# A fused block with a 32-expert MoE: last tile's routing, the bias product in visit 16, a new transfer order in the last visit

## The chip, the cores and the metric

The kernel runs on one core of a Trainium2 chip. The metric is device time in microseconds (us), the median of three runs.

## The reference

One transformer layer in float32, 512 tokens (`SEQ`) of 1024 channels, followed by a final RMS norm:

```
mix = concat(gated_delta_net(h), conformer_conv(h))      h = RMSNorm(x)
x   = x + mix @ w_out
xn  = RMSNorm(x)
x   = x + moe(xn)
out = RMSNorm(x) * final_norm_w

moe: logits = xn @ w_router + b_router;  top 4 of 32, gates = softmax(top values)
     for each token and each of its four experts e:
       gate, up = split(xn @ w_gate_up[e] + b_gate_up[e])
       gate = min(gate, 7); up = clip(up, -7, 7)
       y   += gate_e * (((up + 1) * gate * sigmoid(1.702 * gate)) @ w_down[e] + b_down[e])
```

Each expert has 8 MB of gate and up weights and 4 MB of down weights, which is 403 MB over the 32 experts.

## The kernel before

**The part ahead of the experts** (0 to about 370 us) computes the two mixers. Its last stage is the output projection, `outp`, over four tiles of 128 tokens (t = 0 to 3). PE interleaves it with `xn_turn(t)`, which transposes a finished tile, and `logits(t)`, the router product. For each tile DVE adds the residual (`residual`), ACT takes the norm (`x2_square`, `x2_rstd`), DVE multiplies it in (`normed`, L1386) and picks the top four (`route`): a mask of 32 columns for each token, built by four chained compares (L1410). POOL writes the normed tile to `xn_rows` in DRAM (L613) and splits the gates into three bf16 parts (`split`, L599 to L607).

**Row numbers.** After tile 3, a scan over the masks of all tiles gives each choice's rank among its token's four, a product with a triangular matrix gives its place among its expert's tokens (L2117, L2120), and `hot(e)` compares the places of expert e with the slot numbers (L1502). `idx_mm(e)` multiplies these one-hot matrices by a table of token numbers, gate parts and ranks (L2130), so that DVE's `numbers` gets, for each of 128 slots of the expert, a row of `xn_rows`, a row of the results in DRAM and a gate. It publishes them with `idx_ready`, the queue entry of DVE at L1541. POOL then gathers four groups of 32 slots (`gather`, L624), and DVE transposes what has landed (`first_turn`, `xt_turn`). The semaphore `first_in` counts the first two gathers, `gathered` the others.

**Visits.** An expert is a visit, i = 0 to 31. `gate_up(i)` works in four pairs of weight rows (c = 0, 2, 4, 6) that lie in eight 1 MB slots of `ring`; visit 0 has the rows 4 and 5 in other buffers (`EARLY`). `down(i-1)`, four units (u = 0 to 3) in `dslots`, follows in visit i, so the down work of an expert is done one visit later. After pair 4 PE computes the numbers of visit i+2; visit 1's come after pair 0 of visit 0. DVE turns the result of the products, adds bias and clips; ACT takes the sigmoid (`sigmoid_gate`) and copies the older down results with their gates to `yb` (`results`); POOL scatters them to `y_rows`, four planes of 512 rows in DRAM, one for each rank. Visits 1 to 30 are one loop on each engine. The variable `m` is 30.

**Order of the transfers.** SP issues all weight transfers in a fixed order, each behind a wait on the counter of its buffer: `gu_used` for ring slots, `d_used` for down units. A wait in this queue holds all that stands behind it. SP also waits for `xn_out`, the landing of all normed tiles, ahead of pair 4 of visit 1.

**The last visit.** PE turns the gates (`gates_turn`, L2141) and adds the down bias as a product of gates and `b_down` (`routed_bias(t)`, L2152, with `add_bias(t)` on DVE). These four steps stand behind pair 0, pair 2, the older down units and pair 4. SP issues pairs 0 and 2, both older down pairs, pairs 4 and 6, the last expert's down rows into ring slots 0 to 3, and then the planes back from `y_rows`: the first and second into `dslots` (they need the older down units done), the third into ring slots 4 and 5 (it needs pair 6 and the older scatters), the last into slots 6 and 7 after the last scatters. DVE adds the planes to `hbuf` (L1720), ACT and DVE take the final norm, SP stores. ACT loads the final norm row behind its last results.

## Time and profile before

| | |
|---|---|
| median of 3 runs | 1390.28 us (1388.48 to 1390.84) |
| the profiled execution | 1390.32 us, span 1388.6 us |
| PE matmul busy | 1232.1 us (89%) |
| PE weight load busy | 540.9 us (39%) |
| DVE busy | 683.6 us (49%) |
| ACT busy | 220.4 us (16%) |
| POOL busy | 327.2 us (24%) |
| moved by DMA | 455.33 MB, 328 GB/s in the mean |

The page cuts the span into 40 slices of 34.7 us. The rate of the DMA engines is 252, 339, 401, 410 and 418 GB/s in slices 11 to 15 (347 to 521 us), 424 to 427 in nearly all from 16 to 37, and 379, 409 and 248 in the last three.

How to read it: a busy engine is not by that the one that sets the time. PE is 89% busy over the span, and in the middle the DMA engines are full as well. Which of the two waits for the other is seen in the idle time ahead of a group and in the depth of the queue, the time from the issue of a transfer to its landing. The chain of waits is followed back from the last instruction, so it holds what released each step. In the trace the queue entries of an engine (SPq, DVEq) are its semaphore and DMA instructions.

### The profile page before, as it was taken

Reading aid. Unit: us, or ns where it says so; the run is one execution under the profiler, and the core shown is the slowest. Engines: PE = TensorE matmul, PEld = TensorE weight load, DVE = VectorE, ACT = ScalarE, POOL = GpSimd, SP = SyncE. Lnnn points to the kernel's source line nnn. Section 1 sums busy time; section 2 is a strip of 40 time slices with the busy share of each in tenths; the row PEclk is TensorE's granted clock in tenths of the full one; section 3 lists DMA queues with packets and bytes.
Section 4 is the critical chain, followed back from the end, with each engine's and each line's share of the span. In section 5 each row is a group of like instructions: output and inputs, shape, how many; then the busy total and the mean of one; then the engine's idle time right before and its main releaser. Section 6 shows DMA issues by size and latency. Waiting matters only on the chain.

```text
span 1388.6 us, 32055 instructions
## 1 busy us (share of the span) xinstructions
PE 1232.1 (89%) x12818; PEld 540.9 (39%) x12819; DVE 683.6 (49%) x1365; ACT 220.4 (16%) x435; POOL 327.2 (24%) x435
## 2 busy tenths in 40 slices
PE   6999999999599999799899899788987887879992
PEld 3444555564234443244433334233432332334331
DVE  2898884444543453436433334445443334354428
ACT  3125545313100010000010000000100000001103
POOL 6002111001222233222323222222222222222221
...
GB/s 307 87 61 92 1 31 1 201 73 46 252 339 401 410 418 424 425 427 426 425 426 424 424 427 427 424 427 425 425 424 426 425 426 427 426 425 425 379 409 248
DMA packets 58142, 455.33 MB, mean 328 GB/s; under 512 B 12060, under 2 KB 22356, under 8 KB 32982
## 3 DMA queue, kind: packets, MB, share of 16 engines
...
q14 instruction: 12, 0.10, 0.0%
...
## 4 chain that ended last, share of the span: by engine, by line
PE 53%; DMA 36%; DVE 7%; issue 2%; ACT 2%; POOL 1%; SPq 0%; POOLq 0%; DVEq 0%; ACTq 0%
DMA ring<-in_w_gate_up_dram 26%; PE bank L2166 23%; PE bank L2219 11%; DMA dslots<-in_w_down_dram 8%; PE bank L1826 6%; PE bank L2017 4%; DVE dslots L1145 2%; PE bank L1821 2%; DVE hbuf L1720 1%; PE bank L1894 1%; PE bank L1901 1%; DMA rows<-in_x_dram 1%; DMA wq<-xn_rows,idx_in 1%; PE bank L2152 1%; PE bank L1982 1%
## 5 line engine op out<-in xcount | busy, mean ns | idle before, releaser
L2166 PE MATMUL bank<-ring,wq 128*32 128x512 f32 x4992 | 561.2, 598 | 69.6 <-DMA ring<-in_w_gate_up_dram 66.9
L2166 PEld LDWEIGHTS bank<-ring,wq 128*32 128x32 f32 x4992 | 167.8, 110 | 422.7 <-issue 419.7
L2219 PE MATMUL bank<-dslots,intra 128*32 128x256 f32 x5056 | 281.7, 380 | 24.8 <-DMA dslots<-in_w_down_dram 24.6
L2219 PEld LDWEIGHTS bank<-dslots,intra 128*32 128x32 f32 x5056 | 165.0, 110 | 151.4 <-issue 53.9
L1533 DVE TENSOR_REDUCE small<-bank 128x4 f32<-128x8 f32 x33 | 5.5, 166 | 415.7 <-PE bank L2130 415.7
L1012 ACT ACTIVATE zrows<-intra 128x1024 f32<-128x1024 f32 x31 | 32.8, 1058 | 796.8 <-DVE intra L1626 796.8
L1826 PE MATMUL bank<-hbuf,ring 128*128 128x512 f32 x320 | 148.5, 604 | 0.1
L619 POOL COPY idx_in<-idx 128x4 int32 (+1 forms) x32 | 11.9, 371 | 557.8 <-DVE wq L1511 535.4
L1598 DVE STREAM_TRANSPOSE wq<-bank 128x512 f32<-128x512 f32 x124 | 77.8, 685 | 71.0 <-PE bank L2166 71.0
L624 POOL DMA_INDIRECT wq<-xn_rows,idx_in x82 | 101.7, 1241 | 44.2 <-POOL idx_in L619 27.8
L629 POOL DMA_INDIRECT y_rows<-rows,idx_out x79 | 81.2, 1027 | 55.8 <-issue 43.6
L1145 DVE SCALAR_TENSOR_TENSOR dslots<-dslots,small 128x512 f32<-128x512 f32 x120 | 89.3, 778 | 0.8 <-DVE small L1114 0.2
L1826 PEld LDWEIGHTS bank<-hbuf,ring 128*128 128x128 f32 x320 | 57.3, 190 | 59.3 <-issue 56.3
L1511 DVE STREAM_TRANSPOSE wq<-wq 128x1024 f32<-128x1024 f32 x31 | 63.2, 2040 | 12.6 <-DMA wq<-xn_rows,idx_in 12.6
L1006 ACT ACTIVATE rows<-bank,small 128x256 f32<-128x256 f32 x124 | 48.5, 474 | 93.7 <-PE bank L2219 93.7
L2017 PE MATMUL bank<-ring,dslots 128*128 128x512 f32 x128 | 60.7, 608 | 0.1
L636 POOL DMA_DIRECT2D spare<-in_gdn_dt_bias_dram x93 | 51.8, 566 | 0.1
L1638 DVE SCALAR_TENSOR_TENSOR intra<-zrows,intra 128x1024 f32<-128x1024 f32 x31 | 38.0, 1225 | 27.9 <-PE bank L2219 27.2
L1619 DVE TENSOR_TENSOR zrows<-wq,small 128x256 f32<-128x256 f32 x124 | 44.1, 418 | 0.0
L1502 DVE TENSOR_SCALAR rows<-slot_no,small 128x512 bf16<-128x512 bf16 x136 | 39.1, 351 | 9.8 <-DVE place L1537 9.4
L1619 DVE TENSOR_TENSOR intra<-wq,small 128x256 f32<-128x256 f32 x124 | 43.1, 408 | 0.0
L556 POOL TENSOR_TENSOR sqbuf<-qkbuf 128x512 f32<-128x512 f32 x8 | 11.3, 1416 | 114.2 <-DVE qkbuf L1187 114.2
...
## 6 DMA issues: line engine op xcount, KB each, us to landing
ring<-in_w_gate_up_dram SPq DMA_DIRECT2D x127, 2048.0 KB, 24.9
dslots<-in_w_down_dram SPq DMA_DIRECT2D x61, 2048.0 KB, 25.4
...
dslots<-y_rows SPq DMA_DIRECT2D x2, 2048.0 KB, 20.2
rows<-in_x_dram SPq DMA_DIRECT2D x4, 512.0 KB, 9.8
hbuf<-in_x_dram SPq DMA_DIRECT2D x4, 512.0 KB, 5.5
```

The lines of the kernel that those rows point to most:

```text
L624: pool.indirect_dma_start(out=xg[:, g, :], out_offset=None, in_=xn_q, in_offset=bass.IndirectOffsetOnAxis(ap=numbers[:, g:g + 1], axis=0), ...
L629: pool.indirect_dma_start(out=y_q, out_offset=bass.IndirectOffsetOnAxis(ap=numbers[:, g:g + 1], axis=0), in_=y[:, g, :], in_offset=None, b ...
L636: pool.dma_start(spare[0:1, k * H:(k + 1) * H], gdn_dt_bias[0:1, :]).then_inc(done, 16)
L1006: ins = A(yb[:, g, :], bank[4 + g // 2][:, (g % 2) * QD:(g % 2 + 1) * QD], ACT.Copy, scale=gates[:, bass.ds(stage * GROUPS + g, 1)])
L1145: own.mark(V.scalar_tensor_tensor(out=cacc[:, j, :], in0=ubuf[:, j, k:k + SEQ], scalar=PT[:, j, k:k + 1], in1=cacc[:, j, :], op0=ALU.mult, ...
L1511: V.transpose(xT.rearrange("p g (c s) -> p g c s", c=KC), xg.rearrange("p g (r c) -> p g c r", c=KC)).then_inc(xt_ready, 1)
L1598: V.transpose(hidT[:, g, :, :].rearrange("p h (c s) -> p h c s", c=KC), bank[g][:, :].rearrange("p (h r c) -> p h c r", h=2, c=KC)).then_i ...
L1619: V.tensor_tensor(out[:, g, :].rearrange("p (b s) -> p b s", b=KC), hidT[:, g, half, :].rearrange("p (b s) -> p b s", b=KC), bias.to_broad ...
L1826: ins = M(bank_of(s)[:, :], unit_ap(u)[:, c, half * P:(half + 1) * P], hT[:, c, :], start=(c == 0), stop=(c == KC - 1))
L2017: ins = M(pair[half][:, :], lhs, w, start=(kc == 0), stop=(kc == KC - 1))
L2166: ins = M(bank[g][GROUP * j:GROUP * (j + 1), :], x[:, g, c * GROUP:(c + 1) * GROUP], w[:, :, j * QD:(j + 1) * QD], start=(c == 0), stop=(c ...
L2219: ins = M(b[GROUP * j:GROUP * (j + 1), col:col + QD], actT[:, g, c * GROUP:(c + 1) * GROUP], w[:, cc, j * QD:(j + 1) * QD], start=(c == 0 ...
```

## The change

**Last tile.** Residual and transposition of tile 3 go by halves, and DVE copies both halves of the turned tile, which ACT did for one. The 32 logits come out of one product with `fold_e` instead of a transposition and a reduction on DVE. The mask is one compare over four planes and one reduction with max. Ranks are scanned for each tile, places and one-hot matrices of tiles 0 to 2 are computed ahead of tile 3's norm, and the numbers of visit 0 come from products of three columns (`first_rows`), with the gates in products of their own later (`first_gates`). The rank is now column 2 of the table, the gate parts are columns 3 to 5. In the order listings an index stands ahead of a row as a rule; it is left out here.

**Start of visit 0.** ACT's queue writes the last normed tile to DRAM, counted by `wr_in`. The first gather alone counts `lead_in`; PE starts visit 0 with group 0 (`row_turned`), then group 1, then the others. `split(3)` stands behind the gathers, `hot(1)` behind the first transpositions, and `idx_mm(1)` behind pair 2. SP no longer waits for `xn_out`. SP's queue behind the output projection; L400 and L403 are pairs of gate and up rows, L411 and L414 a down unit, L407 and L410 a down pair. Before:

```order
L422 DMA wq<-in_w_gate_up_dram 128x2048
L400 DMA ring<-in_w_gate_up_dram 128x4096 [waits op_done]
L400 DMA ring<-in_w_gate_up_dram 128x4096 [waits xn_out1,xn_out0]
L411 DMA dslots<-in_w_down_dram 128x2048 [waits gathered,first_in]
L407 DMA dslots<-in_w_down_dram 128x4096
L360 TENSOR_LOAD n_iter [waits route_ready]
```

And now:

```order
L425 DMA wq<-in_w_gate_up_dram 128x2048
L403 DMA ring<-in_w_gate_up_dram 128x4096 [waits op_done]
L403 DMA ring<-in_w_gate_up_dram 128x4096
L414 DMA dslots<-in_w_down_dram 128x2048 [waits gathered,first_in,lead_in]
L410 DMA dslots<-in_w_down_dram 128x4096
L363 TENSOR_LOAD n_iter [waits route_ready]
```

The second ring transfer, pair 4 of visit 1, has lost its wait; the down rows of visit 0 keep theirs. Next PE, from the last logits to the row numbers of visit 1; the outputs `bank` are PSUM banks, `sqbuf` is the gathered and turned input of visit 0. Before:

```order
L2117 MATMUL bank<-kbg,count 128x32 [waits gate_ready]
L2117 MATMUL bank<-kbg,count 128x32 x9
L2120 MATMUL bank<-kbg,count 128x32 x4
L2130 MATMUL bank<-rows 128x6 [waits hot_ready,tg_ready]
L2130 MATMUL bank<-rows 128x6 x15
...
L2166 MATMUL bank<-ring,sqbuf 32x512 [waits slot_in0,xt_ready]
L2166 MATMUL bank<-ring,sqbuf 32x512 x7
...
L2130 MATMUL bank<-rows 128x6 [waits hot_ready,idx_ready]
```

And now:

```order
L2183 MATMUL bank<-rows 128x3 [waits hot_ready]
L2183 MATMUL bank<-rows 128x3 x11
L2104 MATMUL bank<-kbg,count 128x32 [waits gate_ready]
L2104 MATMUL bank<-kbg,count 128x32 x3
L2200 MATMUL bank<-kbg,count 128x32 x4
L2183 MATMUL bank<-rows 128x3 [waits hot_ready]
L2183 MATMUL bank<-rows 128x3 x3
...
L2232 MATMUL bank<-ring,sqbuf 32x512 [waits slot_in0,row_turned]
...
L2191 MATMUL bank<-rows 128x3 [waits tg_ready]
...
L2176 MATMUL bank<-rows 128x6 [waits hot_ready]
```

Behind the mask of tile 3 (`gate_ready`) stand four place products and four number products, where ten and 16 stood; the gates (L2191) and the numbers of visit 1 (L2176) stand inside visit 0, behind pair 0 and behind pair 2.

**Norm row and bias.** `b_down` is loaded after `route_ready` into the buffer of the norm weights, `finw` behind the first sigmoid. The loops are split at visit `MID` = 16, where gates_turn, the four bias steps (one behind each pair) and their adds stand; the numbers of visit 18 come behind them.

**Last visit.** The first two older down units are issued as two transfers behind pair 2, into `convbuf` and `qkbuf`, which are idle by then. PE does pairs 0 and 2, these two units, pairs 4 and 6, the other two units. The last activations go to `qkbuf` and wait for the first two units alone. `results` of the older expert stands between the second and third sigmoid of the last. SP's queue in the last visit (L454 and L460 are the last expert's down rows, the `y_rows` rows the planes). Before:

```order
L400 DMA ring<-in_w_gate_up_dram 128x4096 [waits gu_used]
...
L407 DMA dslots<-in_w_down_dram 128x4096 [waits d_used]
...
L407 DMA dslots<-in_w_down_dram 128x4096 [waits d_used]
...
L400 DMA ring<-in_w_gate_up_dram 128x4096 [waits gu_used]
...
L454 DMA ring<-in_w_down_dram 128x2048 [waits gu_used]
...
L462 DMA dslots<-y_rows 128x4x1024 [waits d_used]
...
L464 DMA dslots<-y_rows 128x4x1024 [waits landed]
...
L467 DMA ring<-y_rows 128x4x1024 [waits scattered]
```

And now:

```order
L452 DMA convbuf<-in_w_down_dram 128x2048
L452 DMA qkbuf<-in_w_down_dram 128x2048
...
L403 DMA ring<-in_w_gate_up_dram 128x4096 [waits gu_used]
...
L410 DMA dslots<-in_w_down_dram 128x4096 [waits d_used]
...
L460 DMA ring<-in_w_down_dram 128x2048 [waits gu_used]
...
L460 DMA ring<-in_w_down_dram 128x2048 [waits landed]
...
L465 DMA dslots<-y_rows 128x4x1024
...
L467 DMA ring<-y_rows 128x4x1024 [waits gu_used]
...
L470 DMA ring<-y_rows 128x4x1024 [waits scattered]
```

One older down pair has become two halves without a wait, the other stands behind pairs 4 and 6; the first plane follows the last down rows without a wait of its own, the second goes into ring slots 4 and 5, the third into 6 and 7.

The diff, cut to its core:

```diff
-        bdn = qkbuf[0:E, 0:D]
+        bdn = ffnw[0:E, :]
+        OLDER = [view(convbuf, 0, 2, D), view(qkbuf, 0, 2, D)]
+        actT_last = view(qkbuf, 0, GROUPS, KC * GROUP)
...
-        PLANES = [view(dslots, 0, T, D), view(dslots, 2 * SLOT, T, D), view(ring, 4 * SLOT, T, D),
-                  view(ring, 6 * SLOT, T, D)]
+        PLANES = [view(dslots, 0, T, D), view(ring, 4 * SLOT, T, D), view(ring, 6 * SLOT, T, D),
+                  view(dslots, 2 * SLOT, T, D)]
...
                 sp.dma_start(EARLY[c], rows_of(0, c)).then_inc(early_in, 16)
             sp.wait_ge(op_done, T)
             gate_up(0, 6)
-            for i in range(2):
-                sp.wait_ge(xn_out[i], 16 * T // 2)
             gate_up(1, 4)
-            sp.wait_ge(first_in, 32)
+            sp.wait_ge(lead_in, 16)
+            sp.wait_ge(first_in, 16)
...
             for c in range(0, KC, 2):
-                if c == 4:
-                    for u in (0, 2):
-                        sp.wait_ge(d_used, m * 4 + (u + 2))
-                        down_pair(None, u)
                 sp.wait_ge(gu_used, m * KC + (c + 2))
                 gate_up(E - 1, c)
+                if c == 2:
+                    for u in range(2):
+                        sp.dma_start(OLDER[u], down_rows(E - 2, u)).then_inc(slot_in[9], 16)
+            sp.wait_ge(d_used, m * 4 + 4)
+            down_pair(None, 2)
             for u in range(4):
-                sp.wait_ge(gu_used, m * KC + (KC + u + 1))
+                if u % 2 == 0:
+                    sp.wait_ge(gu_used, m * KC + (KC + u + 2))
+                if u == 1:
+                    sp.wait_ge(landed, m * 16 + 16)
                 sp.dma_start(view(ring, u * SLOT, 2, D), down_rows(E - 1, u)).then_inc(slot_in[u], 16)
...
-            sp.wait_ge(d_used, m * 4 + 8)
             sp.dma_start(PLANES[0], plane(0)).then_inc(plane_in[0], 16)
-            sp.wait_ge(landed, m * 16 + 16)
+            sp.wait_ge(gu_used, m * KC + (KC + 6))
             sp.dma_start(PLANES[1], plane(1)).then_inc(plane_in[1], 16)
             sp.wait_ge(gu_used, m * KC + 2 * KC)
...
                     split(t - 1)
-                pool.wait_ge(xn_ready, t + 1)
-                pool.dma_start(xn_dram[t * P:(t + 1) * P, :], xn[:, t % 2, :]).then_inc(xn_out[t % 2], 16)
+                if t < T - 1:
+                    pool.wait_ge(xn_ready, t + 1)
+                    pool.dma_start(xn_dram[t * P:(t + 1) * P, :], xn[:, t % 2, :]).then_inc(xn_out[t % 2], 16)
                 if 1 <= t < T - 1:
                     split(t - 1)
...
-                pool.wait_ge(xn_out[i], 16 * T // 2)
-            for g in range(2):
-                gather(g, idx, first_in)
+            pool.wait_ge(xn_out[0], 32)
+            pool.wait_ge(xn_out[1], 16)
+            pool.wait_ge(wr_in, 80)
+            gather(0, idx, lead_in)
+            gather(1, idx, first_in)
             for g in range(2, GROUPS):
                 gather(g, idx)
+            split(T - 1)
...
-            xnT_copy(3)
...
+            act.wait_ge(xn_ready, T)
+            act.dma_start(xn_dram[(T - 1) * P:T * P, :], xn[:, (T - 1) % 2, :]).then_inc(wr_in, 16)
...
+            act.dma_start(finw, final_norm_w.rearrange("(o d) -> o d", o=1).to_broadcast([P, D])).then_inc(
+                late_in, 16)
...
+            with act.Fori(1, MID) as i:
+                visit(i)
             act.wait_ge(gt_done, 1)
             A(GT, bank[7][0:E, :], ACT.Copy).then_inc(gt_copied, 1)
...
+            with act.Fori(MID, m + 1) as i:
+                visit(i)
...
+                if g == 2:
+                    act.wait_ge(d_used, m * 4 + 8)
+                    act.wait_ge(landed, m * 16 + 16)
+                    results((E - 2) % STAGES)
...
-            act.dma_start(finw, final_norm_w.rearrange("(o d) -> o d", o=1).to_broadcast([P, D])).then_inc(
-                late_in, 16)
...
-                own.mark(V.tensor_tensor(x2[:, t, 0:HALF], pair[0][:, :], x2[:, t, 0:HALF], ALU.add))
-                own.mark(V.tensor_tensor(x2[:, t, HALF:D], pair[1][:, :], x2[:, t, HALF:D], ALU.add))
-                own.settle()
-                dve.sem_inc(x2_ready, 1)
+                first = V.tensor_tensor(x2[:, t, 0:HALF], pair[0][:, :], x2[:, t, 0:HALF], ALU.add)
+                if t == T - 1:
+                    first.then_inc(x2_ready, 1)
+                V.tensor_tensor(x2[:, t, HALF:D], pair[1][:, :], x2[:, t, HALF:D], ALU.add).then_inc(x2_ready, 1)
...
-                own.mark(V.tensor_scalar(hits, iota_e, pr4[:, 0:1], None, ALU.is_equal))
-                for k in range(1, TOP_K):
...
-                ins.then_inc(gate_ready, 1)
+                own.mark(V.tensor_tensor(same, iota_e.rearrange("p (o e) -> p o e", o=1).to_broadcast([P, TOP_K, E]),
+                                         pr4.rearrange("p (k o) -> p k o", o=1).to_broadcast([P, TOP_K, E]),
+                                         ALU.is_equal))
+                own.settle()
+                V.tensor_reduce(Msk[:, t, :], same.rearrange("p k e -> p e k"), AX_X, ALU.max).then_inc(gate_ready, 1)
...
+            def ranks(t):
+                now = rank[:, t * E:(t + 1) * E]
+                dve.wait_ge(gate_ready, t + 1)
+                own.mark(V.tensor_tensor_scan(now, ones16[:, 0:E], Msk[:, t, :], 0.0, ALU.mult, ALU.add))
+                own.settle()
+                own.mark(V.tensor_scalar(view(tg, 0, T, E, 6)[:, t, :, 2:3].rearrange("p e o -> p (e o)"), now,
+                                         float(PAST), float(-PAST), ALU.mult, ALU.add))
...
+            hot_tile(0, 0)
+            hot_tile(0, 1)
...
+            dve.wait_ge(lgT_done, T - 2)
+            for half in range(2):
+                dve.wait_ge(xn_turned, T + half)
+                V.tensor_copy(xnT[(T - 1) % 2][:, 4 * half:4 * half + 4, :], view(bank[3 + half], 0, 4, P)
+                              ).then_inc(xnT_half, 1)
+            ranks(2)
+            places(2, 1, 2)
+            hot_tile(0, 2)
...
+            ranks(3)
+            places(3, 1, 3)
+            hot_tile(0, 3)
...
+            dve.wait_ge(idx_done, 1)
+            own.mark(V.tensor_reduce(rowf, first[:, :, 0:2], AX_X, ALU.add))
+            own.settle()
+            V.tensor_scalar(idx[:, 0:GROUPS], rowf, past, None, ALU.add).then_inc(idx_ready, 1)
...
+            dve.wait_ge(lead_in, 16)
+            first_turn(0, 1, row_turned)
+            dve.wait_ge(first_in, 16)
+            first_turn(1, 1, xt_ready)
             dve.wait_ge(gathered, 32)
-            first_turn(1)
...
+            base = (MID - 1) * LOOP_OWN + own.n
+            for t in range(T):
+                add_bias(t)
+            hid_turn(MID + 1)
+            rows_ahead(MID, base)
+            xt_turn(MID + 1)
+            act_part(MID, MID + 1, base + STEPS_IDX)
...
-            for t in range(T):
-                add_bias(t)
             dve.wait_ge(gu_used, m * KC + 2 * KC)
-            dve.wait_ge(d_used, m * 4 + 4)
...
-                if t == T - 1:
-                    pe.wait_ge(xnT_half, 1)
...
-                TR(bank[6][:, 0:P], lgT, ident).then_inc(lg_done, 1)
+                M(bank[6][:, 0:E], lgT, fold_e, start=True, stop=True).then_inc(lg_done, 1)
...
+            def places(t):
+                pe.wait_ge(gate_ready, t + 1)
+                for u in range(t + 1):
+                    ins = M(bank[1][:, t * E:(t + 1) * E], tri16 if u == t else ones16, Msk[:, u, :], start=(u == 0),
+                            stop=(u == t))
+                return ins
...
+            places(1).then_inc(pos_done, 1)
             logits_turn(2)
             outp(3, 12, 16)
+            places(2).then_inc(pos_done, 1)
...
+            def first_rows(t):
+                for g in range(GROUPS):
+                    ins = M(bank[0][:, 3 * g:3 * g + 3], ohv[:, t, g, :], tgv[:, t, 0, 0:3],
+                            start=(t == 0 and g == 0), stop=(t == T - 1), skip_group_check=True)
+                return ins
...
+            pe.wait_ge(hot_ready, T - 1)
+            for t in range(T - 1):
+                first_rows(t)
+            places(T - 1).then_inc(pos_done, 1)
+            for u in range(T):
+                ins = M(bank[7][:, 0:E], ones16, Msk[:, u, :], start=(u == 0), stop=(u == T - 1))
+            ins.then_inc(pos_done, 1)
+            pe.wait_ge(hot_ready, T)
+            first_rows(T - 1).then_inc(idx_done, 1)
...
                         for g in (1,) if by_bank else range(2):
                             ins = gu_mm(c, g, first)
-                        ins.then_inc(gu_used, 1)
+                        ins.then_inc(gu_used, 2 if first and c == 1 else 1)
                     if first and c0 == 0:
-                        pe.wait_ge(idx_ready, 1)
+                        first_gates()
+                    if first and c0 == 2:
                         idx_mm(1, 2 * T + 1)
...
+            pe.wait_ge(row_turned, 1)
...
+            tokens = tokens_left(pe, MID)
+            pe.wait_ge(xt_ready, MID + 2)
+            pe.wait_ge(idx_ready, MID + 2)
+            gates_turn()
+            for t in range(T):
+                gate_up(MID, pairs=(2 * t,), known=tokens)
+                routed_bias(t)
+            pe.wait_ge(acc_ready, T)
+            idx_mm(MID + 2, (MID + 3) * (T + 1) - 1)
+            older_down(MID)
...
-            routed_bias(0)
-            gate_up(m + 1, pairs=(2,), known=tokens)
-            routed_bias(1)
+            gate_up(m + 1, pairs=(0, 2), known=tokens)
             pe.wait_ge(act_ready, m + 1)
             pe.wait_ge(y_ready, m + 1)
-            down(m, tokens_left(pe, m))
-            routed_bias(2)
-            gate_up(m + 1, pairs=(4,), known=tokens)
-            routed_bias(3)
-            gate_up(m + 1, pairs=(6,), known=tokens)
+            older = tokens_left(pe, m)
+            down(m, older, range(2), {0: OLDER[0], 1: OLDER[1]})
+            gate_up(m + 1, pairs=(4, 6), known=tokens)
+            down(m, older, range(2, 4))
```

## Rows read from the trace of the kernel before

**Rows 1.** Windows: length, busy PE, PEld, DVE, ACT, POOL (count); clock; DMA share; GB/s.
```profile
404.00:1304.00 900.00, 807.35 (x9929) 327.75 (x9925) 377.67 (x764) 75.44 (x145) 238.32 (x292) 0.99 1.01 423
...
1316.00:1352.00 36.00, 34.50 (x372) 13.49 (x360) 8.65 (x13) 3.58 (x9) 8.92 (x14) 1.00 1.00 409
```

**Rows 2.** DMA issues (count, KB, us to landing): whole run, then 423 to 428 us.
```profile
ring<-in_w_gate_up_dram SPq DMA_DIRECT2D x127, 2048.0 KB, 24.9
...
dslots<-in_w_down_dram SPq DMA_DIRECT2D x1, 2048.0 KB, 10.0
```

**Rows 3.** Chain of waits (start, length, engine, output, line): routing to visit 1.
```profile
356.49 1.28 DVE convbuf L1386
...
360.27 0.25 DVE kbg L1410
...
361.99 1.24 DVE rows L1502 x4
...
364.63 0.03 DVEq L1541
...
367.09 2.86 DMA wq<-xn_rows,idx
...
371.12 7.67 PE bank L2166 x48
...
385.07 8.95 DMA wq<-xn_rows,idx_in
...
397.12 15.66 PE bank L2166 x144
```

**Rows 4.** Timeline (start, length, engine, line, operation, [idle before <-releaser]): SP, POOL.
```profile
352.57 9.71 SPq L400 DMA_DIRECT2D ring<-in_w_gate_up_dram  x2
...
358.07 0.57 POOL L613 DMA_DIRECT2D xn_rows<-convbuf  x1 [3.98 <-DVE convbuf L1386]
...
365.68 1.11 POOL L624 DMA_INDIRECT wq<-xn_rows,idx  x1 [2.87 <-issue]
...
381.11 1.02 POOL L624 DMA_INDIRECT wq<-xn_rows,idx_in  x1 [0.86 <-POOL idx_in L619]
```

**Rows 5.** DMA issues: the last normed tile (357 to 360 us), the final norm row.
```profile
xn_rows<-convbuf POOLq DMA_DIRECT2D x1, 512.0 KB, 3.8
...
rows<-in_final_norm_w_dram ACTq DMA_DIRECT2D x1, 512.0 KB, 5.7
```

**Rows 6.** Timeline of PE: first matmuls of a pair in visit 16.
```profile
867.03 3.64 PE L2166 MATMUL bank<-ring,wq 128*32 128x512 f32 x32 [1.01 <-DMA ring<-in_w_gate_up_dram]
```

**Rows 7.** Chain of waits: a bias step, older down units, pair 6 of the last visit.
```profile
1321.66 1.91 PE bank L2152 x4
...
1329.05 10.50 PE bank L2219 x192
...
1346.93 3.62 PE bank L2166 x32
```

**Rows 8.** Timeline of ACT, SP and DVE from the older results to the planes.
```profile
1339.70 1.57 ACT L1006 ACTIVATE rows<-bank,small 128x256 f32<-128x256 f32 x4 [19.83 <-PE bank L2219]
...
1340.13 0.41 SPq L464 DMA_DIRECT2D dslots<-y_rows  x1
1351.12 0.36 SPq L467 DMA_DIRECT2D ring<-y_rows  x1
...
1361.07 9.16 DVE L1720 TENSOR_TENSOR hbuf<-hbuf,dslots 128x1024 f32<-128x1024 f32 x8
...
1370.15 4.62 DVE L1720 TENSOR_TENSOR hbuf<-hbuf,ring 128x1024 f32<-128x1024 f32 x4
```

**Rows 9.** Windows: the last pair and the down units of visit 30.
```profile
1304.00:1316.00 12.00, 12.00 (x200) 6.37 (x196) 9.21 (x19) 1.06 (x1) 2.75 (x3) 1.00 0.72 294
```

**Rows 10.** DMA issues: second plane (1340 to 1341 us), third plane.
```profile
dslots<-y_rows SPq DMA_DIRECT2D x1, 2048.0 KB, 22.4
...
ring<-y_rows SPq DMA_DIRECT2D x1, 2048.0 KB, 17.0
```

216 lines of the change are left out of this document (111 added, 105 removed).

## The prediction

> **What bounds the kernel now.** I read the windows of the long middle first. From 404 us to 1304 us the 16 DMA engines are busy with a share of 1.01 and move 423 GB/s, while PE is busy 807 of 900 us; over 1316 to 1352 the share is again 1.00 [rows 1]. So from visit 2 on the stream of expert weights sets the pace. The issue rows say how deep its queue is: a pair of weight rows lands 10.0 us after its issue in visit 1, but 24.9 us in the median over the run [rows 2]; that is five transfers of 2 MB. Three things can therefore move the end: when the stream starts, how many bytes it carries, and what follows the last bytes. Work of PE, DVE or ACT in the middle is free as long as it is shorter than the queue.
>
> The chain of waits around routing tells when the stream starts [rows 3]. Residual, norm and router of tile 3 run in series, the norm at 356.49, the mask complete at 360.52, the row numbers published at 364.63; then two gathers, landed at 369.95, the turn and the first matmul at 371.12. PE is not the limit again until 397.12: visit 1's gathers take until 394.02. From there pairs are freed by PE and the stream is full. At the end [rows 7, 8] PE goes through routed bias and last visit until 1350.55, and DVE then adds planes without a pause from 1361.07.
>
> **The change, part by part.** The sum is made against the profiled execution, 1390.32 us (span 1388.6, so 1.7 outside), which is 0.04 above the median.
>
> *Last tile.* DVE copies half of the turned tile while it waits, which makes the logits some 1.0 us earlier, but rank, product and one-hot of tile 2 (some 1.2 us in five short operations) now stand ahead of the norm, which so starts at about 356.5 as before. After it the reduction of the logits goes (0.24 us) and four serial compares of 0.25 become one compare and one reduction of 0.28 each: 0.7 us. From mask to numbers took 4.1 us (360.52 to 364.63); a quarter of the scan, one one-hot instead of four (1.24 us for four [rows 3], so 0.9 less), four matmuls instead of 16, one reduction fewer and no place ahead of the numbers leave some 2.1 us. Numbers are ready at about 361.8, 2.8 us early. For tiles 0 to 2 the same work goes where DVE waits for PE.
>
> *What the gathers wait for.* They also need the last normed tile in DRAM. It is written at 358.07 and landed after 3.8 us, and SP held back pair 4 of visit 1 until then: its two issues span 352.57 to 362.28 [rows 4, 5]. Now both pairs, 4.2 MB, go at 352.6 and 352.9. At 423 GB/s, from a first byte near 353.4, they last until 363.3, and the 0.5 MB of the tile end with them at about 364.5. Bounds for the tile's landing: 3.8 us as before (361.7), and 8.95 us, which the gathers needed among weights [rows 3] (366.8); the norm row at the end, of the same size and among fewer transfers, took 5.7 us [rows 5]. I take 365.0. The first gather then goes at 366.0 against 365.68 [rows 4]: the 2.8 us are gone, +0.3.
>
> The Trainium skill (DMA: Bandwidth & Descriptors, "Queues, rings and completion order") says an engine empties a packet of some 9 to 17 descriptors of one ring before it turns to the next ring. No row here shows that order; it is the third rival below.
>
> *One gather opens visit 0.* Before, two had to land (369.95) and the turn took 1.2 us till PE started. Now one: 366.0, some 2.5 us to landing (2.86 for the second one before [rows 3]), 0.6 for half the turn: PE starts at 369.1, 2.0 us early. All four land at about 372.2, 0.3 late, and so do the down rows of visit 0 that SP queues behind that wait; nobody needs them before 418.
>
> *Visit 1's numbers move back.* Their 16 matmuls came after pair 0 (371.12 + 7.67 = 378.79 [rows 3]); now gates stand there (0.5 us) and they follow pair 2: 369.1 + 7.6 + 0.5 + 5.3 + 0.5 = 383.0, so visit 1's gathers are issued from 384.9 instead of 381.11 [rows 4], the last at 388.9. That speaks against the change. But the old ones landed at 394.02 only because weights drained till then: they are bounded by the drain, which ends about 1.5 us earlier, since pair 0's and pair 2's slots come free 1.5 to 2 us earlier. I take 392.5. Transposes and the first bank turn take 3.1 us as before (394.02 to 397.12): visit 1 starts at 395.6, **1.5 us early**. Bounds: PE's own path (369.1 + 24.2 + 0.5 + 1.2 = 395.0, a gain of 2.1), and a landing 8.95 us after the last issue (397.9, a start at 401.0, a loss of 3.9).
>
> *Final norm row in visit 1.* 0.5 MB, 1.2 us of the stream at 423 GB/s; visit 1 still has short pauses, so **+0.8** (bounds 0 and 1.2).
>
> *Bias in visit 16.* Four times 1.91 us [rows 7], 0.5 of transposes and 1.4 for the last add: 10 us of PE in visit 16. There PE waits for weights before each pair, 1.0 us in the row shown [rows 6], and transfers land some 24 us after issue, so the stream doesn't notice: 0. If the queue were dry it would be the full 10 us.
>
> *End.* The PE path loses 8.2 us of bias (1350.55 to 1342.4). It gains less, since weights then bind it. Transfers land there as the queue lets them: the second plane, issued at 1340.13, after 22.4 us, at 1362.5; the third, issued at 1351.12, after 17.0, at 1368.1, 5.6 us behind it [rows 8, 10]. The mean share falls to 0.72 between 1304 and 1316 [rows 9] although transfers are queued, so some engines are ahead and idle while others lag and never pause; filling the gap doesn't help those. Bytes and their number are the same in the new order (two halves, pairs 4 and 6, the second down pair, last down rows), so I keep the series, late by the 0.8. The last activation needs pair 6 (some 1340) and only down units 0 and 1, so DVE is through it by about 1352.5, where it was 1361.07: it now waits for planes. Plane 1 at 1363.3 plus four adds (4.6 us, [rows 8]) is 1367.9; plane 2 lands at 1368.1 + 0.8 - 1.2 (the norm row no longer runs beside it) = 1367.7. Third plane's adds start at 1367.9 against 1370.15: **-2.25**, the 0.8 within. Behind them the last plane, norm and store stay.
>
> The older results are 8 us later: down units 2 and 3 end at 1347.5 (5.25 us, half of [rows 7]), ACT copies till 1349.1; from the end of the copies (1341.27) to SP's third plane were 9.85 us [rows 8], so its issue is at 1359.0, ahead of 1362.5 when the plane before it lands. Covered by 3.5 us.
>
> Sum: -1.5 - 2.25 = -3.75: **1386.6 us**.
>
> **Rivals.** (2) *The start gains nothing.* Visit 1's gathers, issued 3.8 us later, land 1 to 4 us later than I say. Start 0 to +2, end -2.25: 1388.1 to 1390.1, say 1388.8. For: 8.95 us under load; against: their weights go earlier too. (3) *The tile's write passes pair 4.* If it follows pair 6 at once, it lands after 3.8 us as before, at 361.7, the first gather goes at 362.8, PE starts 5 us early and visit 1, then bound by its gathers, 4 us early: 1390.3 - 4.0 - 2.25 = 1384.1. That is what the skill's packets would give. Against: gathers of some KB took 8.95 us among weights. (4) *The lag is made up at the end.* The window from 1304 to 1316 leaves 0.28 of 12 us unused, 3.4 us [rows 9]; were it usable, planes landed that much earlier, and the third, issue bound, at about 1366: 1384.6. (5) *Slower: third plane too late.* Its issue hangs on down units 2 and 3, copies and scatters. If scatters take longer than 13.3 us instead of 9.85, each us is lost; if the plane needs 17.0 us from issue as before, it lands at 1376.0, DVE starts 5.9 us later than before, less 1.5: 1394.7. For: this chain moved by 8 us; against: the 17.0 us were queueing behind two planes. (6) *Visit 16 isn't hidden*: up to 10 us, 1396.6, if queue depth has shrunk below 10 us; 24 us speak against.
>
> **Chances.** Forecast 0.42, (2) 0.25, (3) 0.10, (4) 0.08, (5) 0.10, (6) 0.05. A measurement here can tell about 0.2% (2.8 us), so faster means below 1387.5. Three quarters of the forecast lie there (the bounds of the start reach across): 0.32 + 0.18 = 0.50. Same: 0.10 + 0.25 = 0.35; slower 0.15. Range: from between (3) and (4), 1383.8, to the slow end of (2) with the norm row at its full cost, 1390.8; (5), (6) and what lies below are left out.
>
> **What would show it.** Numbers ready near 361.8 but the first gather at about 366 (at 363 for rival 3); the first matmul at 369.1; visit 1 at 395.6; a share of 1.01 through visit 16 with bias matmuls in it; DVE waiting before each plane, its third set of adds at 1366.4 (1367.9 less 1.5). Wrong if the tile's write lands within 4 us of its issue, if visit 1 starts after 397.1, or if the third plane's issue comes after the second's landing.

## The result, and the profile after

The changed kernel takes 1393.58 us in the median of 18 runs (1391.3 to 1395.31), against 1390.32 for the kernel before (18 runs): a ratio of 1.0024, 95% interval 1.0017 to 1.0031. It is 3.3 us slower. I had forecast 1386.6, and a range that ended at 1390.8. The profiled execution took 1393.55 us, span 1391.8, so that it stands 3.2 us behind the one of before.

First the long middle. The windows of the changed kernel, columns as in [rows 1]:

```profile
404.00:1304.00 900.00, 817.59 (x9932) 323.80 (x9928) 382.31 (x769) 77.44 (x147) 239.17 (x292) 0.99 1.01 422
1304.00:1316.00 12.00, 12.00 (x176) 5.34 (x172) 6.96 (x16) 0.00 (x0) 0.17 (x1) 1.00 1.01 427
1316.00:1352.00 36.00, 30.18 (x410) 14.01 (x406) 13.29 (x31) 3.46 (x7) 7.97 (x12) 1.00 0.97 401
```

Share and rate are those of before in the middle; PE is busy 10 us longer in it, as the bias moved there. The time did not go there. The chain of waits from the last tile to visit 1 shows where it went [rows 3]:

```profile
357.04 8.82 DMA xn_rows<-convbuf
...
366.82 2.90 DMA wq<-xn_rows,idx
...
370.43 7.46 PE bank L2232 x48
...
389.96 5.33 DMA wq<-xn_rows,idx_in
```

The last normed tile took 8.82 us to land, in place of 3.8 [rows 5]. The row numbers were ready at 360.78, but the first gather, which also needs the tile, went at 366.82. PE started visit 0 at 370.43, 0.7 us earlier than before, and visit 1's last gather landed at 395.29, 1.3 us later. The timelines of SP and then PE over the same stretch and on to visit 2:

```profile
352.17 0.80 SPq L403 DMA_DIRECT2D ring<-in_w_gate_up_dram  x2
373.11 0.33 SPq L414 DMA_DIRECT2D dslots<-in_w_down_dram  x1
...
407.34 0.35 SPq L403 DMA_DIRECT2D ring<-in_w_gate_up_dram  x1
...
398.33 17.35 PE L2232 MATMUL bank<-ring,wq 128*32 128x512 f32 x144 [3.26 <-DVE wq L1625]
...
432.71 2.78 PE L2232 MATMUL bank<-ring,wq 128*32 128x512 f32 x24 [0.51 <-issue]
```

The same rows of the kernel before:

```profile
402.74 0.35 SPq L400 DMA_DIRECT2D ring<-in_w_gate_up_dram  x1
...
397.12 15.66 PE L2166 MATMUL bank<-ring,wq 128*32 128x512 f32 x144 [1.76 <-DVE wq L1598]
...
428.93 6.64 PE L2166 MATMUL bank<-ring,wq 128*32 128x512 f32 x60
```

Visit 1 starts 1.2 us late, its first 144 products take 1.7 us more, and visit 2 starts 3.8 us late (432.71 after 428.93). The other 0.9 us come behind these products: the older down units take 0.25 us more, and a pause of 0.51 us stands ahead of visit 2, for which the profile shows no releaser. The windows say why the products are slower (PE's granted clock is the third number from the end):

```profile
396.00:398.00 2.00, 0.00 (x0) 0.00 (x0) 2.00 (x3) 0.00 (x0) 0.00 (x0) 1.00 0.68 287
398.00:400.00 2.00, 1.67 (x12) 0.58 (x16) 1.96 (x6) 0.00 (x0) 0.00 (x0) 0.65 1.02 434
400.00:402.00 2.00, 2.00 (x16) 0.48 (x11) 1.81 (x9) 0.00 (x0) 0.79 (x2) 0.50 0.49 209
402.00:404.00 2.00, 2.00 (x24) 0.63 (x20) 1.97 (x6) 0.19 (x1) 1.64 (x2) 1.00 0.21 66
```

PE had been idle for 3.26 us. Its clock falls within the first of these products (0.65 is the mean of 398 to 400), is at 0.50, the 1.2 GHz level, until 402, and is back at 1.00, the 2.4 GHz level, after that. Before, the pause was 1.76 us and the clock stayed at 1.00. From visit 2 on the distance hardly changes: the numbers in visit 30 are computed at 1305.13 after 1301.34, 3.8 us apart.

Now the end. The lines are PE's timeline of the older down units 2 and 3, SP's issue of the third plane with its time to landing, and DVE's three sets of adds [rows 8, 10]:

```profile
1345.10 4.09 PE L2292 MATMUL bank<-dslots,intra 128*32 128x256 f32 x70 [1.11 <-DMA dslots<-in_w_down_dram]
1351.17 1.70 PE L2292 MATMUL bank<-dslots,intra 128*32 128x256 f32 x25 [1.98 <-issue]
...
1364.39 0.36 SPq L470 DMA_DIRECT2D ring<-y_rows  x1
...
ring<-y_rows SPq DMA_DIRECT2D x1, 2048.0 KB, 9.0
...
1359.98 4.63 DVE L1760 TENSOR_TENSOR hbuf<-hbuf,dslots 128x1024 f32<-128x1024 f32 x4 [1.60 <-DMA dslots<-y_rows]
1365.80 4.63 DVE L1760 TENSOR_TENSOR hbuf<-hbuf,ring 128x1024 f32<-128x1024 f32 x4 [1.20 <-DMA ring<-y_rows]
1373.38 4.63 DVE L1760 TENSOR_TENSOR hbuf<-hbuf,ring 128x1024 f32<-128x1024 f32 x4 [2.95 <-DMA ring<-y_rows]
```

DVE now waits ahead of each plane. The third set starts 3.2 us later than before (1370.15), which is the whole difference. Against a stream that is 3.8 us late, the new end has given back 0.6 us in this execution.

### The profile page after: what moved, and what is told of

It reads as the page before. It is cut to its first block, busy times and chain, and to the rows that moved or that the text cites. A ratio compares the mean times of both kernels' runs of the same rounds, so it can differ in the third digit from the quotient of the medians.

```text
span 1391.8 us, 32047 instructions
## 1 busy us (share of the span) xinstructions
PE 1236.1 (89%) x12838; PEld 534.9 (38%) x12839; DVE 682.6 (49%) x1359; ACT 220.6 (16%) x434; POOL 326.6 (23%) x434
## 4 chain that ended last, share of the span: by engine, by line
PE 55%; DMA 34%; DVE 5%; issue 3%; ACT 2%; POOL 1%; SPq 0%; POOLq 0%; DVEq 0%; ACTq 0%
PE bank L2232 24%; DMA ring<-in_w_gate_up_dram 20%; PE bank L2292 12%; DMA dslots<-in_w_down_dram 11%; PE bank L1866 6%; PE bank L2057 4%; DVE dslots L1154 2%; PE bank L1861 2%; PE bank L1934 1%; PE bank L1941 1%; DMA ring<-y_rows 1%; DMA xn_rows<-convbuf 1%; DMA rows<-in_x_dram 1%; PE bank L2218 1%; PE bank L2022 1%
## 5 line engine op out<-in xcount | busy, mean ns | idle before, releaser
L2232 PEld LDWEIGHTS bank<-ring,wq 128*32 128x32 f32 x4992 | 159.5, 111 | 419.4 <-issue 414.1
L1016 ACT ACTIVATE zrows<-intra 128x1024 f32<-128x1024 f32 x31 | 32.8, 1059 | 792.5 <-DVE intra L1653 740.5
```

The source lines that it names most:

```text
L2232: ins = M(bank[g][GROUP * j:GROUP * (j + 1), :], x[:, g, c * GROUP:(c + 1) * GROUP], w[:, :, j * QD:(j + 1) * QD], start=(c == 0), stop=(c ...
```

## The experiments

The kernel before was timed again beside each of the kernels below, and its median lay between 1389.2 and 1390.0 us. So where a microsecond matters, the ratio to it is compared and not the median. An interval is about 0.9 thousandths (1.2 us) to either side, 1.3 in e2, e6 and e8, which have the fewest runs. Rows and times within a run are from its one profiled execution.

**e1. SP's wait for the last tile put back** (on the changed kernel).

```diff
             gate_up(0, 6)
+            sp.wait_ge(xn_out[0], 32)
+            sp.wait_ge(xn_out[1], 16)
+            sp.wait_ge(wr_in, 80)
             gate_up(1, 4)
```

> Changed kernel, with one thing put back: SP waits until the last normed tile is in DRAM before it issues pair 4 of visit 1. In the changed kernel that tile took 8.8 us to land (357.04 to 365.86), against 3.8 us before. Theory A (the write shares the engines with 4 MB of weights that were issued ahead of it, and that eats the shorter routing): the tile lands 4 us after its issue, near 361, the first gather goes near 362, PE starts visit 0 near 366 instead of 370.4, visit 1 near 395; time about 1389.5 us. Rival (pair 4 of visit 1 issued some 9 us later starves the stream instead): PE starts early, but visit 1 does not end earlier and the time stays at 1393.6 us or above.

Measured: 1390.2 us, ratio 1.0004 (0.9995 to 1.0013). The loss is gone, but not in the way that I expected. The tile landed after 3.7 us, and the gather went at 362.58, four microseconds early. It then ran beside pair 4, issued 1 us ahead of it, and took 7.41 us. Its chain, and PE in visit 1:

```profile
362.58 7.41 DMA wq<-xn_rows,idx
...
390.98 2.74 DMA wq<-xn_rows,idx_in
...
396.82 15.66 PE L2235 MATMUL bank<-ring,wq 128*32 128x512 f32 x144 [0.72 <-DVE wq L1628]
```

PE started visit 0 at 370.71, no earlier than in the changed kernel. What did move is SP: it issued the first down rows at 370.94 and not at 373.11. Visit 1's last gather then landed 2.74 us after its own issue, at 393.72, PE waited 0.72 us and kept its clock.

**e2. The norm row back at the end** (changed kernel; `act.dma_start(finw, ...)` behind the last results, as before).

> Changed kernel, with the load of the final norm row back at its old place behind the last results. In the changed kernel it is issued at 403.82, in a stretch in which no weights are queued, and SP issues pair 0 of visit 2 at 407.34, some 2 us after PE freed the slots by my reckoning. Theory (the norm row stands in the way of that issue or of its bytes): SP issues within 0.5 us of the slots being free, and the time falls by 1.2 to 2 us, to about 1392 us. Rival (the row fills a stretch in which the engines are idle anyway, and SP is late for another reason): SP is as late as before and the time stays at 1393.6 us, less at most 0.3.

Measured: 1394.45 us, ratio 1.0030 (1.0018 to 1.0043). SP issued pair 0 of visit 2 at 408.28, where PE had begun visit 1 at 399.39: as late as with the row in visit 1. The row costs nothing that can be told, and SP's lateness has another cause.

**e3. Visit 1's numbers in the middle of pair 2** (changed kernel).

```diff
                             ins = gu_mm(c, g, first)
+                        if first and c == 2:
+                            idx_mm(1, 2 * T + 1)
...
-                    if first and c0 == 2:
-                        idx_mm(1, 2 * T + 1)
```

> Changed kernel, with the row numbers of visit 1 computed in the middle of pair 2 of visit 0 instead of behind it, which issues visit 1's gathers some 2.6 us earlier (383.4 instead of 385.98). Theory B (these gathers set the start of visit 1, and PE's wait for them of 3.26 us also halves its granted clock until 402.4, which costs 1.7 us more): visit 1 starts near 396.5, its clock stays at 1.00, and the time falls by 3 us or more, to about 1390.5 us. Rival (the gathers land when the weights ahead of them have drained, whenever they are issued): the last one lands at 395.3 as in the changed kernel, and the time stays at 1393.6 us.

Measured: 1393.88 us, ratio 1.0026 (1.0016 to 1.0036), the rival's number. PE had started visit 0 0.98 us later in this execution (371.41), so that the last gather went at 389.85, no more than 0.1 earlier by the clock, 1.1 earlier against PE. It landed at 397.19, 1.9 later:

```profile
389.85 7.34 DMA wq<-xn_rows,idx_in
```

Here SP issued the first down rows at 374.07 and not at 373.11. The landing went with them rather than with the gathers' issue. The test is weaker than planned, since the issue hardly moved.

**e4. The pause ahead of visit 1 filled** (changed kernel).

```diff
                         idx_mm(2, 3 * T + 2)
+                        for _ in range(12):
+                            M(bank[7][:, 0:P], ident, ident, start=True, stop=True)
```

> Changed kernel, with 12 idle products of the 128x128 identity behind the numbers of visit 2, in the gap in which PE waits 3.26 us for visit 1's input; they change no result. It prices the clock alone: visit 1 starts at 398.3 as in the changed kernel. Theory C (the clock fell to half because of the gap, and the 1.7 us that PE loses in pair 0 of visit 1 delay the stream): the granted clock stays near 1.00 from 398 to 402 us, and the time falls by 1.5 to 2 us, to about 1392 us. Rival (the stream makes these 1.7 us good by visit 4): no change, 1393.6 us. If the clock falls all the same, the gap is not what lowered it.

Measured: 1391.44 us, ratio 1.0012 (1.0003 to 1.0021). That is 2.1 us less than the changed kernel by the medians and 1.7 by the ratios (1.0024), with 1.6 to either side. Visit 1 started at 398.06, its 144 products took 15.66 us, and visit 2 started at 430.80, 1.9 us earlier than in the changed kernel. The windows, to be laid beside those of the changed kernel:

```profile
398.00:400.00 2.00, 1.95 (x21) 0.70 (x24) 1.82 (x7) 0.00 (x0) 0.02 (x1) 1.00 0.92 393
400.00:402.00 2.00, 2.00 (x24) 0.60 (x20) 1.96 (x8) 0.00 (x0) 1.15 (x2) 1.00 0.63 266
```

The clock is at 1.00, and up to there visit 1 differs by no more than a start 0.3 us earlier. So the pause lowered the clock, and this cost about 1.7 us that was not made good later. The Trainium skill (TensorE: Matmul & The Clock Gate, "What's actually happening") says that a gate sets the clock by how busy PE has been lately; this pair of runs agrees.

**e5. The new end alone** (kernel before with the bias in visit 16, the norm row in visit 1 and the new last visit; routing and start as before).

```diff
+            with pe.Fori(1, MID) as i:
+                visit(i)
...
+            down(m, older, range(2), {0: OLDER[0], 1: OLDER[1]})
+            gate_up(m + 1, pairs=(4, 6), known=tokens)
+            down(m, older, range(2, 4))
```

> Kernel before, with the bias in visit 16, the norm row in visit 1 and the new last visit, and nothing of the new routing or the new start. Theory D (the loss of the change sits in the start, and the new end gains little, since the third plane is issued only when the older expert's late scatters have landed: 1364.39 in the changed kernel, 9.0 us ahead of its adds at 1373.38): visit 1 starts at 397.1 as before, the third set of adds starts near 1369.6 against 1370.15, and the time is 1389.8 us, within 0.5 of before. Rival (the end gains 2.25 us as I predicted, and the changed kernel's loss at the start spoilt it): 1388.1 us.

Measured: 1389.24 us, ratio 0.9995 (0.9986 to 1.0004). It is 4 us faster than the whole change (0.9995 against 1.0024). So the loss is in the routing and the start. The end alone gives 0.7 us here (from 1.9 us gained to 0.6 lost), so the 2.25 of the forecast lies outside what this run allows. In the profiled execution visit 1 started at 395.49 and not at 397.1, after a pause of 0.64 us.

**e6. Pair 4 of visit 1 behind the gathers** (changed kernel).

```diff
             gate_up(0, 6)
-            gate_up(1, 4)
             sp.wait_ge(lead_in, 16)
             sp.wait_ge(first_in, 16)
             sp.wait_ge(gathered, 32)
+            gate_up(1, 4)
```

> Changed kernel, with pair 4 of visit 1 moved on SP from ahead of the waits for visit 0's gathers to behind them. With the pair ahead of all, the tile's write took 8.8 us and the gather 2.9; with the pair issued at 361.59, right ahead of the gather, the write took 3.7 and the gather 7.4: either way PE starts visit 0 at 370.4 to 370.7. Theory E (the pair's 2 MB are in the way of whichever small transfer runs beside them): write and gather both take 3 to 4 us, the first gather lands near 365.5, PE starts near 366.2, visit 1 starts near 393, and the time falls to about 1386 us. Rival (the pair's bytes, sent 18 us later, are missed: the engines idle from 358 to 370, and visit 1's gathers then queue behind them): PE starts early but visit 1 no earlier than 396, and the time is 1390 us or above.

Measured: 1395.1 us, ratio 1.0036 (1.0023 to 1.0050). The first half of theory E held: the write took 3.7 us, the gather 2.9, and PE started at 366.94. Then 5 MB that had been kept back stood ahead of visit 1's gathers:

```profile
366.94 7.21 PE L2232 MATMUL bank<-ring,sqbuf 128*32 128x512 f32 x48 [5.31 <-DVE sqbuf L1535]
...
399.31 18.39 PE L2232 MATMUL bank<-ring,wq 128*32 128x512 f32 x144 [7.98 <-DVE wq L1625]
```

PE waited 7.98 us ahead of visit 1, and the lower clock then cost 2.7.

**e7. The bias in visit 16 alone** (kernel before).

```diff
-            routed_bias(0)
...
+            for t in range(T):
+                gate_up(MID, pairs=(2 * t,), known=tokens)
+                routed_bias(t)
```

> Kernel before, with the bias product and its adds in visit 16 and nothing else of the change; the last visit keeps its order, without the four bias steps. Theory F (the bias is hidden in visit 16, as the changed kernel shows: PE is 8.7 us late in visit 17 and on its old distance from visit 20 on; and the last visit gives back some of its 8.2 us, up to the landing of the planes): the third set of adds starts near 1368, and the time is about 1388 us, less than that of the whole new end. Rival (the landings of the planes set the end, and nothing is gained): 1390.2 us.

Measured: 1389.66 us, ratio 0.9995 (0.9986 to 1.0004). Visit 16 hides the bias; what the last visit gives back is 0.7 us, and at most the 1.9 that the interval lets through.

**e8. The first down rows earlier** (changed kernel: SP waits for the first gather alone).

```diff
             sp.wait_ge(lead_in, 16)
-            sp.wait_ge(first_in, 16)
-            sp.wait_ge(gathered, 32)
```

> Changed kernel, with SP's wait for all four gathers of visit 0 ahead of the first down rows cut to the wait for the first gather alone. In the changed kernel SP issues these 3 MB at 373.11, after 9 us in which the engines are busy 0.30 to 0.37 of the time; before it was 371.94. Theory G (visit 1's gathers land when the weights ahead of them have drained, 395.30 after 394.02, and the drain is as late as this wait makes it): the rows go at 370, the last gather lands at 392 to 393, visit 1 starts at 396 to 396.5, where PE allows it, with its clock at 1.00, and the time falls by 3 us, to about 1390.5. Rival (the other three gathers of visit 0 now run among weights and take 7 us, so PE stalls in pair 0 for what is gained): 1393 us or above.

Measured: 1396.37 us, ratio 1.0052 (1.0039 to 1.0065). The last gather of visit 0 took 7.90 us among the rows, and PE stood still in pair 0:

```profile
380.91 4.11 PE L2230 MATMUL bank<-ring,sqbuf 128*32 128x512 f32 x24 [4.18 <-DVE sqbuf L1533]
```

Visit 1 started at 402.99. The engines look idle while SP waits there, and still the wait pays for itself.

**e9. Pair 4 and the down rows behind the first gather** (changed kernel; `gate_up(1, 4)` behind `lead_in`, the two other waits out).

> Changed kernel, with pair 4 of visit 1 and the first down rows both issued when the first gather has landed, not when all have. The run with the pair behind all gathers started PE 3.5 us earlier (366.94), yet visit 1 at 399.31, because 5 MB were issued only from 369.44 on. Theory G (what counts is when the bytes ahead of visit 1's gathers are issued): issue at 366.1, drained 3.4 us earlier, the last gather lands near 393, visit 1 starts near 394 and PE keeps its clock: about 1387.5 us. Rival (gathers 1 to 3 of visit 0 take 7 us among weights and PE stalls there): visit 1 starts at 397 or later and the time is 1391 us or above.

Measured: 1391.13 us, ratio 1.0011 (1.0003 to 1.0020). PE started at 364.97 and stood still for 3.86 us behind a gather of 7.75. Visit 1 began at 397.58, and again at the lower clock, after a pause of only 1.86 us:

```profile
397.58 17.35 PE L2230 MATMUL bank<-ring,wq 128*32 128x512 f32 x144 [1.86 <-DVE wq L1623]
```

**e10. The last visit's old order** (changed kernel, bias still in visit 16).

```diff
-            down(m, older, range(2), {0: OLDER[0], 1: OLDER[1]})
-            gate_up(m + 1, pairs=(4, 6), known=tokens)
-            down(m, older, range(2, 4))
+            down(m, tokens_left(pe, m))
+            gate_up(m + 1, pairs=(4, 6), known=tokens)
```

> Changed kernel, with the order of the last visit as before (both older down pairs between pairs 2 and 4, planes in their old buffers, older results ahead of the sigmoids); the bias stays in visit 16. It prices the new order alone. The bias alone gave 0.4 us and the whole new end 0.8 us on the kernel before, so by these the new order is worth 0.4 us here: 1394.0 us. Theory D (the third plane's issue hangs on the older expert's late scatters, 1364.39, so that the new order gains nothing): 1393.0 to 1393.6 us. Rival (the new order is what earns 2.25 us, as I predicted): 1395 us or above.

Measured: 1392.23 us, ratio 1.0022 (1.0013 to 1.0030), within the interval of the changed kernel. Here no gain of 2.25 us hangs on the new order.

**e11. The kernel before with the down rows earlier** (`sp.wait_ge(gathered, 32)` out).

> Kernel before, with SP's wait ahead of the first down rows cut from all four gathers of visit 0 to the first two. Nothing else is changed. Theory G (SP's wait there sets the drain that visit 1's gathers end with): the rows are issued near 370 instead of 371.94, the gathers of visit 1 land near 392.5 instead of 394.02, visit 1 starts near 396 and the time falls by 1 us, to about 1389.2. Rival (PE or the gathers themselves set visit 1's start): 1390.2 us.

Measured: 1394.25 us, ratio 1.0029 (1.0019 to 1.0038). The ratio rises by 0.0029, where e8's rose by 0.0028. The last gathers again ran among weights. PE paused for 1.22 us inside pair 0, until 376.18, and its clock was still at 0.50 up to 380, where it had risen at 376 in the kernel before. Visit 1 started at 399.22.

**e12 to e15. Idle products in visit 0's wait, first place.** Four kernels got products of the identity ahead of `gate_up(0, ...)`, behind PE's wait for `route_ready`: 18 in the kernel before (e14) and the new end alone (e12), 26 in the changed kernel (e13, with 10 more in the pause ahead of visit 1) and in the changed kernel with SP's wait (e15). The expectations stand in the order e14, e12, e13, e15.

```diff
             tokens = tokens_left(pe, 0)
+            for _ in range(18):
+                M(bank[4][:, 0:P], ident, ident, start=True, stop=True)
```

> Kernel before, with 18 idle products in PE's wait for visit 0's gathers and nothing else. Theory H: the first pair of visit 0 takes 5.3 us instead of 7.67, and the time falls by about 2 us, to 1388 us. Rival: the gathers of visit 1 land at 394 as before, and the time stays at 1390.

> Kernel before with the bias in visit 16 and the whole new last visit (1389.24 us), and 18 idle products of the identity in the 7.5 us in which PE waits for visit 0's gathers; they change no result. In the kernel before the granted clock is 0.50 from 360 to 374 us, and the first pair of visit 0 takes 7.67 us where later ones take 5.3. Theory H (that clock costs 2.3 us of PE's way to visit 1, and the stream follows PE there): first pair 5.3 us, visit 1 starts 2 us earlier, time about 1387.2 us. Rival (visit 1's gathers and the weights ahead of them set visit 1's start, whatever PE does): 1389.2 us.

> Changed kernel, with 26 idle products in its wait of 9.4 us for visit 0's first gather and 10 in its gap ahead of visit 1. Filling the second gap alone gave 2.1 us (1391.44). Theory H: the first pair takes 5.3 us instead of 7.46, visit 1's numbers and gathers come 2 us earlier, and the time is about 1389.5 us. Rival (the drain of the weights issued from 373.1 on decides, so an earlier PE only waits longer ahead of visit 1): 1391.4 us.

> Changed kernel with SP's wait for the last normed tile put back (1390.2 us), and 26 idle products in PE's wait for visit 0's first gather. Theory H: 1388 us, the same 2 us as on the kernel before, so that what is left between this and the kernel before is the new end's 0.8 us less the norm row. Rival: 1390.2 us.

Measured, in the same order: 1391.94 (ratio 1.0019), 1389.53 (1.0002), 1391.48 (1.0016) and 1389.74 us (1.0006), each 0.9 thousandths to either side. They missed their aim: in e14 the products ran from 368.64 to 374.46 and held the first pair up by what the clock gave back. Why e14 is slower than the kernel before, by more than its interval, no run tells.

**e16 to e18. Idle products in visit 0's wait, second place**, ahead of `pe.wait_ge(route_ready, 1)`: kernel before (e16, 18 products), new end alone (e17, 18), and changed kernel with SP's wait (e18, 24).

> Kernel before, with 18 idle products right behind visit 0's numbers, ahead of PE's wait for the visit counts. In e14 they stood behind that wait (368.6 to 374.4), so that they held the first pair up by 3 us and gave all of it back: pair 0 took 5.29 us, but from 374.4. Now they should run from 363.4 to about 370. Theory H: pair 0 of visit 0 starts at 371.1 and takes 5.3 us, visit 0 ends at 392.5 instead of 394.8, visit 1 starts near 395, the time falls by 2 us to about 1387.5. Rival (drain): visit 1's gathers land at 394 as before, visit 1 starts at 397 after a longer wait, and the time is 1389.4 us or, with a lowered clock there, 1391.

> The same idle products at the same place in the kernel before with the bias in visit 16 and the new last visit (1389.24 us without them). Theory H: 1387.2 us. Rival (drain): 1389 us or above.

> The changed kernel with SP's wait for the last normed tile put back (1390.2 us without them), and 24 idle products right behind visit 0's numbers, from about 361 to 369. Theory H: the first pair takes 5.3 us instead of 8.2, visit 1 starts near 395, and the time is about 1388 us. Rival (drain): visit 1's last gather lands at 393.7 as without them, PE waits longer, and the time is 1390 us or above.

Measured: 1391.17 (ratio 1.0010, 1.0001 to 1.0019), 1389.1 (1.0000, 0.9991 to 1.0009) and 1390.95 us (1.0005, 0.9996 to 1.0014). None is faster than without the products; e16 is 1.4 us slower, just beyond its interval. On the kernel before they did what they should up to visit 1:

```profile
394.64 17.34 PE L2168 MATMUL bank<-ring,wq 128*32 128x512 f32 x144 [1.65 <-DVE wq L1598]
```

Visit 0 ended 2.3 us early, its slots came free earlier, visit 1's gathers landed at 391.56 and visit 1 started 2.5 us early. After a pause of 1.65 us the clock was lower, and visit 2 started at 429.02, where it had been 428.93. The 2.5 us went in three pieces: 1.7 by the clock, 0.4 in the older down units, and 0.35 in a pause ahead of visit 2. In e17 the clock stayed up after a pause of 1.44 us, but visit 1 was no earlier (395.79, against 395.49 in e5): SP issued the first down rows at 373.03 and not at 371.15, and the last gather landed at 392.70, 0.4 us later than in e5. So an earlier end of visit 0 is not enough; the gathers of visit 1 and the clock must follow. In e18 the clock had fallen again by the first pair, which took 7.05 us.

**All profiles together.** From the start of visit 1 to the start of visit 2 it is 31.8 us in the profiled execution of the kernel before, and 32.6 to 32.8 us in all 19 others, less what the lower clock cost there. So up to visit 2 PE's own work carries the delay, and no weights are waited for. The execution of the kernel before is also the only one without a pause ahead of visit 2, so that some 0.9 of the 3.8 us may be its luck. Past it, the profiled execution's time less the start of its visit 2 separates start and end. It is 961.0 to 962.9 us (mean 961.9) in the four kernels with the old end, 960.4 and 960.6 in the two with the bias in visit 16 and the old order (e7, e10), and 958.3 to 961.2 (mean 959.8) in the 14 with the whole new end. Visit 2 starts at 428.3 to 429.3 in the kernel before, e5 and e7, which share the old start, and at 432.7 to 433.9 in the changed kernel, e2 and e10, which share the new one. By these the start costs some 4.6 us (means 433.4 and 428.8), and the end gives some 2.1 back, 1.3 of it by the bias and 0.7 by the order. Visit 2's start ranges over 7.5 us in the 14 kernels and the rest over 2.9, so the start is carried through to the end. The size of the end is less sure, since these are single executions: those of e5, e12 and e18 ran 1.9 to 2.5 us below the median of their kernel. By the medians, which do not have this fault, the new end gives 0.7 us in e5 (1.2 to either side), 2.4 in e12 beside e14 and 2.1 in e17 beside e16 (both 1.8 to either side). The bias alone gives 0.7 (e7), and the order adds nothing in e5 beside e7 nor in the changed kernel beside e10. So the end is worth some 1 to 2 us, and the split between bias and order stays open.

## Why the prediction was wrong

The result lies outside the range, beyond my second rival, which stopped at 1390.1. Two steps failed: the late down rows, which I had put at nothing, and the term that was missing, what a longer pause does to PE's clock. Step by step:

*Last tile.* Right, and a little too careful: numbers at 360.78, where I had said 361.8.

*What the gathers wait for.* Right in mechanism and size: the tile landed at 365.86 (I had said 365.0). The rival that it lands in 3.8 us fell: the write took 8.8 or 8.9 us in each of the changed kernel, e2 and e3. The engines' time shows how. ACT's queue, which carries the tile, moved nothing from the issue at 357.04 until 360. Then it had 14 to 22% of the engines' time in each microsecond up to 364, and SP's queue with the weights 62 to 110%. The Trainium skill (DMA: Bandwidth & Descriptors, "Queues, rings and completion order") has the engines take turns between queues, a packet at a time. The trace agrees that both queues are served from 360 on, but not that the small write gets through early.

*One gather opens visit 0.* 370.43 instead of 369.1: the gather went 0.8 us later than I said and DVE and PE took their time.

*"Nobody needs them before 418".* This is the first step that failed. I saw that SP's down rows would go late, asked only who reads them, and put their lateness at nothing. They were also what stood ahead of visit 1's gathers in the engines: they were issued at 373.11 after 371.94, and the last gather landed at 395.29 after 394.02, 1.2 and 1.3 us later. In the runs this landing followed the issue of the rows after 21.1 to 23.1 us, as long as SP's waits there were kept and PE's first pairs stood where they had (before, after, e2 to e5, e7, e10, e12 to e14). That it follows them is read from these runs; no run moved the rows alone, since e8 and e11 also put gathers of visit 0 among weights. In e1 the engines were free by then, and the last gather landed in 2.74 us.

*Visit 1's numbers move back.* I took 392.5 for the last landing. It came at 395.29; the drain did not end 1.5 us earlier, it ended later. My slow bound had a start at 401.0, so the working held the case. The range did not: it went no further than rival (2), in which the start loses at most 2 us.

*What a later start does.* This term was missing. The sum counted the delay of visit 1 and no more. PE's pause grew from 1.76 to 3.26 us, the clock fell to 0.50, and the first pairs took 1.69 us longer. Of visit 2's 3.8 us the two failed steps make 2.9 (1.21 and 1.69), and the other 0.9 came behind them, may be the luck of one execution, and has no cause that a run shows. The row with the falling clock was there before: 7.67 us for the first pair of visit 0 [rows 3], where 5.3 is usual. Filling the pause gave back 1.7 us by the ratios (e4).

*SP in visit 2.* PE ended visit 1's first pair at 405.2 in the changed kernel; SP, which waits for that, issued at 407.34. It was 1.6 to 2.2 us late in the changed kernel, e2, e4, e9 and e16, and 0.4 to 1.0 in the kernel before, e1, e5, e14 and e17. What held it is not in the profile, and no run tells: it was as late without the norm row (e2). It did not hold visit 2 up, which started as far behind visit 1 in e4 as in e1.

*Norm row.* I forecast 0.8 us; no cost was found (e2).

*Bias in visit 16.* Right in its size, nothing. PE was 8.7 us late by visit 17 (906.00 after 897.26) and back on its old distance in visit 20. What PE waited for changed with it; the waits of PE over visits 16 and 17, changed kernel and kernel before:

```profile
PE bank L2292 <- issue: 6.7, 4, 2.6
PE bank L2232 <- issue: 2.3, 3, 1.0
```

```profile
PE bank L2166 <- DMA ring<-in_w_gate_up_dram: 8.5, 6, 2.2
PE bank L2219 <- DMA dslots<-in_w_down_dram: 5.4, 4, 1.7
```

In place of 13.9 us for weights it waited 9.0 us for nothing that the profile shows. Without the stream's slack these would have been a cost of their own.

*End.* I had -2.25. In the one profile of the changed kernel it was -0.6, over all of them -2.1, and by the medians between -0.7 and -2.4. So the size may have been right, but my account of it was not. I had put the third plane's issue at 1359.0; it was 1364.39, 1.6 us more than the stream's delay explains. The older units 2 and 3 took from 1345.10 to 1353.1 instead of 5.25 us, with a pause of 1.98 in them that the profile puts down to nothing, and the plane then landed 9.0 us after its issue, not behind its forerunner. Rival 5 had this mechanism; its price was smaller than I had said, since the plane took 9.0 us from its issue and not 17.0. The last activations were late as well: DVE was through them at 1358.4 and not at 1352.5, after a wait of 3.51 us for ACT, which copied the older results in between (1353.20). What share of the gain comes with the bias alone I had not separated, and the runs leave it open.
